# Decode stage of a hybrid decoder step: four row groups for the outer products, column groups for the k/q and attention products, and a fixed step for every piece

## The reference

```
# SSD, 16 heads of 64 rows x 128 columns, per sequence b
h   = h * exp(dt*A) + outer(dt*x, B)        # new state
y   = (C . h) + D*x
# gated DeltaNet (GDN), 8 heads of 128 x 128, per sequence b
S   = S * exp(g)
vn  = beta * (v - k . S)                    # k, q normalised
S   = S + outer(k, vn)
y   = q . S
# memory attention, 4 heads, 256 tokens, per sequence b
p   = softmax(q . K / sqrt(128));  y = p . V
```

## Time and profile before

| | |
|---|---|
| median of 3 runs | 1452.47 us (1449.58 to 1455.79) |
| profiled execution | 1452.82 us, of which the trace's span is 1450.9 us |
| PE matmul busy in the span | 1351.4 us (93%) |
| mean granted TensorE clock | 0.982 of full speed |
| decode stretch (from the end of the prompt's GDN work to the last projection matmul) | 887.9 to 1183.9 us: 296.0 us |

### The profile page before, as it was taken

How to read it: one execution, slowest core, us unless ns; L and a number is a source line. 1 busy time by engine, 2 the same in 40 slices (tenths; PEclk the granted TensorE clock), 3 DMA queues, 4 the chain that set the end, 5 groups by cost and what they waited for, 6 DMA issues and landing times.

```text
span 1450.9 us, 25445 instructions
## 1 busy us (share of the span) xinstructions
PE 1351.4 (93%) x10652; PEld 1292.0 (89%) x10652; DVE 738.1 (51%) x1040; ACT 558.5 (38%) x992; POOL 474.7 (33%) x424
## 2 busy tenths in 40 slices
PE   6999998899999999999999999899899979999993
PEld 6999998888898999989899899898896979999993
DVE  7754434555457474656547541568662154233224
ACT  6653333432354545454443543232112162233221
POOL 3030003333535253444435454785221041010003
PEclk9999999999999999999999999999999999999997
DMA  7324342112111121111111114245444414333322
GB/s 279 101 88 130 118 131 88 44 44 59 59 59 47 46 59 41 50 46 59 46 60 61 60 44 133 73 151 169 161 159 163 158 59 132 116 111 110 111 65 118
DMA packets 38819, 138.14 MB, mean 95 GB/s; under 512 B 4449, under 2 KB 5857, under 8 KB 38449
## 3 DMA queue, kind: packets, MB, share of 16 engines
q1 hardware_dynamic: 30384, 109.80, 24.1%
q10 hardware_dynamic: 8208, 26.22, 5.2%
q0 software_dynamic: 112, 0.50, 0.1%
HBM read 121.25 MB, written 15.24 MB: 94 GB/s over the span
## 4 chain that ended last, share of the span: by engine, by line
PE 69%; DVE 10%; issue 10%; POOL 5%; ACT 5%; DMA 1%; DVEq 0%; ACTq 0%; POOLq 0%; SPq 0%
PE ps L753 33%; PE ps L1056 15%; PE ps L645 13%; POOL w_lo L1946 3%; PE ps L701 2%; DVE conv_a L1628 2%; PE ps L705 2%; PE ps L1026 1%; ACT w_hi L1083 1%; PE ps L1009 1%; ACT L1083 1%; DVE h_lo L1503 1%; DVE fin L1934 1%; DVE d_v L1871 1%; DVE w_lo L1481 1%
## 5 line engine op out<-in xcount | busy, mean ns | idle before, releaser
L753 PE MATMUL ps<-h_hi,w_hi 128*128 128x260 f32 x1920 | 421.6, 301 | 26.8 <-DVE w_lo L1481 11.2
L753 PE MATMUL ps<-h_lo,w_hi 128*128 128x260 f32 x1920 | 390.0, 285 | 0.0
L753 PE MATMUL ps<-h_hi,w_lo 128*128 128x260 f32 x1920 | 389.8, 285 | 0.0
L1083 ACT ACTIVATE w_hi<-w_raw 128x512 fp32r<-128x512 f32 x352 | 213.2, 624 | 445.8 <-PE ps L753 254.2
L753 PEld LDWEIGHTS ps<-h_hi,w_hi 128*128 128x128 f32 x1920 | 301.2, 192 | 40.5 <-issue 32.1
L753 PEld LDWEIGHTS ps<-h_lo,w_hi 128*128 128x128 f32 x1920 | 300.1, 191 | 0.0
L753 PEld LDWEIGHTS ps<-h_hi,w_lo 128*128 128x128 f32 x1920 | 299.8, 191 | 0.0
L1946 POOL TENSOR_TENSOR w_lo<-w_raw,w_hi 128x512 fp32r<-128x512 f32 x152 | 206.9, 1365 | 270.7 <-ACT w_hi L1083 270.1
L1481 DVE TENSOR_TENSOR w_lo<-w_raw,w_hi 128x512 fp32r<-128x512 f32 x200 | 149.1, 767 | 234.3 <-ACT w_hi L1083 233.6
L1056 PE MATMUL ps<-y_hi,w_hi 128*128 128x260 f32 x640 | 129.0, 283 | 9.6 <-DVE y_lo L1918 5.6
L1056 PE MATMUL ps<-y_lo,w_hi 128*128 128x260 f32 x640 | 129.3, 283 | 0.0
(11 more groups left out here) (334 smaller groups left out, 1913.6 us busy)
## 6 DMA issues: line engine op xcount, KB each, us to landing
w_raw<-in_w_in SPq DMA_DIRECT2D x120, 512.0 KB, 3.6
w_raw<-in_w_out SPq DMA_DIRECT2D x40, 512.0 KB, 3.6
w_raw<-in_w_mem SPq DMA_DIRECT2D x16, 512.0 KB, 3.5
x_t<-in_x_t SPq DMA_DIRECT2D x8, 520.0 KB, 7.7
fin<-in_x_t SPq DMA_DIRECT2D x8, 520.0 KB, 4.5
out_y_t<-fin SPq DMA_DIRECT2D x8, 520.0 KB, 2.7
d_st<-in_st_ssd ACTq DMA_DIRECT2D x8, 512.0 KB, 4.5
out_s_ssd<-d_st ACTq DMA_DIRECT2D x8, 512.0 KB, 3.3
```

The source lines that it names most:

```text
L753: last = mm(out[:, hf, :], w[:, g % 2, P * (at_k % 8):P * (at_k % 8) + P], a[:, at_k, HALF * hf:HALF * hf + HALF], start=(at_k == 0 and j ...
L1083: return nc.scalar.activation(out, in_, func, **more)
```

## The change

The list `late` and its pauses are gone. Every decode piece gets a fixed step, counted from the start of tile 43 (`DEC_AT`), and the projection of tiles 19 to 58 is one run of items into which they are put. The last pieces stand at steps 201 to 218, in tiles 55 and 56; the eight SSD pieces follow each other every 7.5 steps from step 13 on, the four GDN pieces start at steps 82, 96, 113 and 127, the attention products at 140 to 168 and 183 to 201. Some loads are issued two steps behind the product that frees their buffer.

```diff
-POOL_TILES = (12, 50)
+POOL_TILES = (12, 46)
+DEC_AT = [(-40, "zero"), (-34, "bcols")] + [(9.8 + 0.2 * i, ("load", i)) for i in range(4)]
+DEC_AT += [(10, "consts"), (12, "bcast"), (13.2, "dtx"), (14.4, "rows"), (16, "gzero"), (17.4, ("cb", 0)), (34, "gcols"), (46.4, ("cb", 1)),
+           (60.2, "grows"), (62.6, "gss"), (63.4, "grk"), (65.2, "gcoef")]
+for _i in range(8):
+    DEC_AT += [(13 + 7.5 * _i, ("decay", _i)), (19.2 + 7.5 * _i, ("outer", _i)), (20.4 + 7.5 * _i, ("add", _i)), (22.2 + 7.5 * _i, ("ymul", _i)),
+               (23.6 + 7.5 * _i, ("store", _i)), (24.6 + 7.5 * _i, ("yred", _i)), (30.4 + 7.5 * _i, ("load", _i + 4))]
+for _t, _kq in enumerate((82, 96, 113, 127)):
+    DEC_AT += [(_kq, ("kq", _t)), (_kq + 2.2, ("vn", _t)), (_kq + 4.6, ("gouter", _t)), (_kq + 6.6, ("gadd", _t))]
...
+for _b, (_k, _v) in enumerate(zip((140, 142, 154, 156, 158, 160, 166, 168), (183, 184.2, 185.4, 186.6, 195, 197, 199, 201))):
+    DEC_AT += [(_k, ("attk", _b)), (_k + 2, ("load", 20 + _b)), (_v, ("attv", _b)), (_v + 2, ("load", 28 + _b))]
```

On PE, the rows dt*x, B, C, k and v are now turned by transposes into tiles whose rows lie in four groups of 32 partitions, with masks that make B and C block-diagonal for two sequences (`b_diag`, `c_diag`) and vn for four (`d_vbd`). An outer product is then four matmuls, each from one row group and into a PSUM bank of its own:

```diff
+                elif step == "outer":
...
+                    for j in range(4):
+                        last = one(side[j][:, 0:2 * P], dtx_rows[32 * j:32 * j + 2, i, :], b_diag[32 * j:32 * j + 2, i // 4, :, :].rearrange("p i n -> p (i n)"))
+                    last.then_inc(sem("d_outer"), 1)
...
+                    for i in range(4):
+                        for j in range(4):
+                            last = mm(side[0][32 * j:32 * j + 8, 0:P], kq_sel[:, t, j, i, :], d_st[:, (2 * t + i // 2) % 4, 4 * (i % 2) + j, :],
+                                      start=i == 0, stop=i == 3)
...
+                    for j in range(4):
+                        last = one(side[j], kq_rows[32 * j:32 * j + 4, t, :], d_vbd[32 * j:32 * j + 4, :, :].rearrange("p i v -> p (i v)"))
...
+                    for h in range(MEM_H):
+                        last = mm(side[0][32 * h:32 * h + DB, 0:MEM_T], q_sel[:, h, DB * b:DB * b + DB],
+                                  d_st[:, b % 4, 2 * h:2 * h + 2, :].rearrange("p m t -> p (m t)"), start=b == 0, stop=b == DB - 1)
...
+                    for m in range(2):
+                        for h in range(MEM_H):
+                            last = mm(side[3][32 * h:32 * h + DB, 0:P], p_sel[:, m, h, DB * b:DB * b + DB], d_st[:, b % 4, 4 * m + h, :],
+                                      start=(b == 0 and m == 0), stop=(b == DB - 1 and m == 1))
```

On POOL the outer product is gone; the decay stays, and seven memsets come in (two at step -40). On DVE the adds read the product from PSUM:

```diff
+                    V.tensor_tensor(st, st, ps[:, 4:8, 0:2 * P].rearrange("p j (i n) -> p j i n", i=2), ALU.add).then_inc(sem("d_new"), 1)
...
+                    V.tensor_tensor(by_group(d_tmp[:, :, :]), by_group(d_st[:, i % 4, :, :]), d_cb[:, :, :, :], ALU.mult).then_inc(sem("d_ymul"), 1)
```

More of the change, by code:

```diff
@@ L163, in spread, with spread_ssd @@
         upto = (i + 1) * len(side) // len(main)
-        out += [s for s in side[done:upto] if s != PAUSE]
+        out += side[done:upto]
         done = upto
     return out
-def paced(side):
-    out = []
+def spread_ssd(main, side):
+    padded = []
     for it in side:
-        step = f"{it[0]} {it[-1]}" if it[0] in ("ssd", "gdn", "att", "atty", "decgdn") else it[0]
-        out += [PAUSE] * PAUSES.get(step, 0) + [it]
-    return out
+        padded += [None] * (it in (("ssdend",),) or it[0] == "ssd" and it[2] == 1) + [it]
+    return [it for it in spread(main, padded) if it]
 def proj_items(first, last):
@@ L215, in timeline @@
     start = proj_items(a, b)
[L216 removed]
+    items += start[:FIRST] + spread_ssd(start[FIRST:], side)
     phases = {}
@@ L229, in timeline @@
     assert not phases
[L230 to L238, removed]
     items += spread(proj_items(NTILE - 1, NTILE), [("yhi", e) for e in range(ET - 4)])
     items += [("ylo", 0), ("ylo", 1), ("post", NTILE - 1, 0), ("post", NTILE - 1, 1), ("post", NTILE - 1, 2), ("ylo", 2), ("ylo", 3), ("out", 0, 0), ("post", NTILE - 1, 3),
-              ("out", 0, 1), ("post", NTILE - 1, 4), ("out", 0, 2), ("decgate", 2), ("ylo", 4), ("ylo", 5)]
+              ("out", 0, 1), ("post", NTILE - 1, 4), ("out", 0, 2), ("dec", "gate", 2), ("ylo", 4), ("ylo", 5)]
     items += spread([("out", 0, e) for e in (3, 4, 5)], [("yhi", e) for e in range(ET - 4, ET)])
@@ L444, in build @@
[L444 to L449, removed]
-    d_sv = r_side.place("d_sv", [P, 4])
-    d_n = r_side.place("d_n", [P, 2, ET, DB])
+    kq_cols = r_side.place("kq_cols", [P, 4, P])
+    d_vbd = at("d_vbd", [P, 4, P], F32, r_side.next - 4 * 4 * P)
+    kq_rows = r_side.place("kq_rows", [P, 4, P])
+    bv_rows = r_side.place("bv_rows", [P, 4, P])
@@ new lines, in build @@
+    d_diag = at("d_diag", [P, 320], F32, r_side.next)
+    d_sel = at("d_sel", [P, P], F32, r_side.next + 320 * 4)
+    d_tmp = r_side.place("d_tmp", [P, DB, P])
+    d_rq = r_side.place("d_rq", [P, GDN_H * DB])
+    d_dx = r_side.place("d_dx", [P, 8, DB])
+    d_sv = r_side.place("d_sv", [P, 4])
+    assert r_side.next <= r_side.start + (ET - 1) * NT * 4
+    r_b.reset()
+    s_cols = r_b.place("s_cols", [P, 12, P])
+    kq_sel = r_b.place("kq_sel", [P, 4, 4, 4, 8])
+    v_cols = at("v_cols", [P, 4, P], F32, conv_u_at)
@@ L503, in across, with groups, by_group, pairs_of @@
         return ap.unsqueeze(1).to_broadcast([ap.shape[0], m, ap.shape[1]])
+    def groups(t):
+        return t.rearrange("p (j r) -> p j r", r=32)
+    def by_group(ap):
+        return ap.rearrange("p (i j) n -> p j i n", j=4)
+    def pairs_of(ap):
+        return ap.rearrange("p h b -> p (h b)").rearrange("p (t i j) -> p t j i", t=4, j=4)
+    def cols_of(tile, first):
+        return tile.rearrange("p t (j r) -> p t j r", r=32)[:, :, :, first:first + 4]
     def chunk(c):
```

656 lines of the change are left out of this document (370 added, 286 removed).

## The result

The changed kernel takes 1387.97 us (median, 1386.41 to 1391.25), the kernel before 1452.09 in the same comparison: a ratio of 0.957 (95% interval 0.955 to 0.959). The forecast was 1421 with a range of 1395 to 1456, so the sign was right and the size was not: the change brings twice what was forecast, and more than the low end of the range.

What follows compares the result with a forecast made beforehand. PE was taken to set the pace, with 105.4 us of its 296.0 us decode stretch open to change; -18.9 + 3.4 - 9.3 - 5.0 - 2.0 = -31.8 took 1452.8 to 1421 us, range 1395 to 1456.

Steps and rivals of the forecast that it cites:

- decode products: Small decode matmuls on PE: partial overlap of row and column groups, 53.1 us in place of 72.0, -18.9.
- tile shapes: PE's changes of tile shape: 35 bursts of small tiles in place of 17, at 0.19 us each, +3.4.
- PE's waits: PE idle in the decode stretch: 20.3 us falls to 11 (range 4 to 20), -9.3.
- clock: TensorE clock in the decode stretch: fewer waits, fewer falls, half of the loss stays, -5.0 us.
- the end: Last tile: norm and gates move to tiles 55 and 56, off ACT while it rounds y, -2 us.
- the first term: Decode matmuls on PE: 46.1 us for six sums, between 23.2 (complete overlap) and 77.6 (none); -18.9 in all.
- The signs named for it: Chain pieces in the trace: `outer` at 1.15 right, 0.84 or 1.84 wrong; `attk` 1.15 against 0.46 or 1.84.
- The rival of complete overlap: Decode products on PE: groups overlap completely, 22.9 us less and 2 of waits back, 1400 us; chance 20%.
- the fourth term: TensorE clock: fewer waits bring fewer falls and half of the loss stays, -5.0 us (0 to -10).
- Groups that take turns: Decode products on PE: each group waits for the one before, +12.6, 1467 us; half of no overlap's 18%.
- no-change variant: Decode products on PE: no overlap, but waits fall as forecast, 1452.6 us; half of no overlap's 18%.
- Waits that move to DVE: SSD part: DVE takes POOL's place, splits come late, third and fourth terms (waits, clock) are lost, 1435 us; chance 17%.

Runs made afterwards that it cites:

- one group: Changed kernel with all four products of each set reading row group 0 or writing column group 0: 1450.18 us, ratio 0.999.
- by turns: Changed kernel with each outer product issued three times, group after group: 1392.37 us, ratio 0.959; for k/q products, the changed kernel's own order, 1387.97 us.
- in pairs: Changed kernel with k/q products issued two of one column group in a row, then the next group's, twice round: 1392.72 us in one execution.
- six in a row: Changed kernel with each outer product issued three times, six instructions for one row group before the next group's: 1410.72 us, ratio 0.972.
- the moved splits: Kernel before with GpSimd splitting low parts up to tile 46 instead of 50: 1456.95 us; changed kernel with the limit back at 50: 1389.14 us.
- A regular spread of the pieces: Changed kernel with decode pieces in the same order but at even distances from step 9.8 to 239.5: 1383.77 us, ratio 0.953.
- eight in a row: Changed kernel with k/q products issued eight instructions per column group and value products four, before the next group's: 1390.99 us, ratio 0.958.

## Why the prediction was wrong

Terms of the sum as the forecast had them, and as the two profiled executions show them:

| term | forecast (its bounds) | measured |
|---|---|---|
| decode products | -18.9 (-41.8 to +12.6) | 72.0 to 29.5: -42.5 |
| tile shapes | +3.4 | +2.4 |
| PE's waits | -9.3 (-16.3 to 0) | 20.3 to 3.5: -16.8 |
| clock | -5.0 (0 to -10) | 9.9 to 1.9: -8.0 |
| the end | -2 (0 to -4) | 0 |
| sum | -31.8 | -64.9 |

(29.5 is 23.5 for the six sums and about 6 for transposes and small products; the shapes are what is left, 231.1 - 190.6 - 29.5 - 3.5 - 1.9 = 5.6 in place of 3.2.)

**The step that failed** is the choice of a value between the bounds of the first term. The bounds were right at both ends: 77.6 without overlap (77.3 measured with one group) and 23.2 with complete overlap (23.5 measured), the lower one in part by luck. The ten bursts of `cb` and `outer` took 6.5 where it had 8.4, since it let the weight loads of the four groups follow each other, and in the trace they start within 0.02 us and last 0.18; the other bursts took 17.0 where it had 14.8, for the fixed part of each. I took 46.1, by the assumption that the second instruction of a product, which goes to the same group as the first, holds back the next group's. The signs named for it decide: `outer` 0.65, under even the 0.84 of the best case, and `attk` 0.55 against 0.46 and 1.15. The runs by turns, in pairs and in a row show what holds instead: an instruction for a busy group doesn't hold back what is behind it until four stand for the same group, one running and three waiting. With the order of the change (never more than two in a row) the limit never comes into play. So PE does not keep strictly to program order between groups, though the opening section says so of every engine: with six in a row the second group's first starts 0.54 us after the burst's start, the first group's fourth at 0.75.

The Trainium skill, TensorE: Matmul & The Clock Gate, Part 3 (Packing small matmuls), says that matmuls start and end strictly in program order. As a rule for when they start, the traces don't agree with it: eight instructions in two lengths and a fixed part leave no room for the third to wait behind the second. Its measured 3.07 for four row groups, with 512 columns, is near to what the runs gave: 1.92 / 0.65 = 2.95 for `outer`, with 256 columns, and 3.62 / 1.07 = 3.4 for `gouter`, with 512. Column groups gave 1.82 / 0.55 = 3.3 and 3.59 / 0.99 = 3.6.

**The rival of complete overlap** was the right mechanism, but at 1400 it was too slow by 12: 9.5 of that are waits (3.5 measured, where it kept the forecast's 11 and added 2 for DVE), 3 are the clock. DVE was hardly late: the add is 1.22, POOL or not, and the multiplication fell from 1.85 to 1.41, so seven and a half steps have some 5.9 us of DVE work where I had 6.4 (and 7.2 at worst), in PE's 6.3. The waits named one by one were over-counted: loads 3 and the vn chain 2 gave nothing, POOL's splits 0.3 for 2, DVE's splits 1.5 for 3 (and 1.0 for an add). That the waits go without the overlap too (0.15 us with one group) makes them a term of their own. Which part of the change takes them away is not separated: the moved splits and the steps set by hand are out, and the outer products that left POOL, `vn` in two operations and the new order of the pieces remain.

**The clock** was put down to waits alone in the fourth term. Its loss fell by 8.0 in place of 5.0, and the run with one group has next to no waits and loses 14 us to the clock. So falls stand behind a gap in PE's work and also, with no gap, behind bursts of products with two or four rows; shortening the bursts, which the first term counted only by its own length, kept the clock up as well. The kernel before has a fall of the second kind too: in the first window of the earlier trace rows PE is busy for all of its 29.9 us and the clock is 0.94. It falls behind the burst of 3.68 at 900.83, products with 8 rows (their row, then the window behind them):

```profile
L645 PE MATMUL ps<-ident_r,d_tmp 8*128 8x8 f32 x32 | 3.7, 252 | 0.0
```

```profile
905.00:910.00 5.00, 5.00 (x32) 5.00 (x31) 0.15 (x1) 0.41 (x1) 1.29 (x1) 0.66 0.34 105
```

Its other falls stand beside waits, and how its 9.9 divide was not tried.

**The end** gave nothing: the last roundings of y still come after the last projection, and the part behind the decode stretch is as long as before (267.2 us, and 267.0 before).

**The rivals that lost.** Groups that take turns: no, though its no-change variant, 1452.6, is what the kernel with one group gives (1450.18), so that part of the working stands: products up, waits down, nothing gained. Waits that move to DVE: 1.5 and 1.0 us in place of the 14.3 that this rival priced. The Trainium skill's rule on PSUM Bottleneck (TensorEngine Tiling (Array Packing)) is not seen in these traces: the add that reads PSUM kept to 1.20 to 1.22 us. What the rival said of DVE's splits is seen in the kernel before with the moved splits, where they came late and cost 6.7 us of waits.

**The range** ended at 1395, without the fast edge of the case of complete overlap, and that case itself kept the forecast's waits and clock, though products and clock go together here: shorter bursts leave fewer falls of the clock. Its low end should have been the sum of the best ends, 1452.8 - 41.8 + 3.4 - 16.3 - 10 - 4 = 1384.

## What to carry to other kernels

Small fp32 products between big ones are worth putting into four row or column groups: here 77 us of them became 24 (the products that they replaced were 72 with the small ones), issued by turns, so that no more than four instructions in a row go to one group. Where the bounds of an overlap are far apart, a value between them needs a row that shows it; without one, the forecast should be given as two cases, and effects that hang on the same cause (here the length of the bursts and the clock) should be summed within a case. A regular spread of the pieces did as well as steps set by hand.

## What the runs showed of the hardware that I had not expected

- Order within a burst: 32 instructions of 128 columns took 0.99 us by turns, 1.01 in pairs of products and 2.31 eight in a row; 24 of 256 columns took 1.51 by turns and 3.11 six in a row. In both runs in a row the next group starts when three instructions of the group before have yet to start, so a limit of four for each group, one running and three waiting. What makes this limit stays open.
- The clock without a gap in PE's work: behind most bursts of 3.1 to 3.7 us of products with two, four or eight rows, and behind three of ten of 1.92 us, it fell from 2.4 to 1.2 GHz for a few microseconds; behind bursts of 3.59 with 128 rows and 8 weight columns it stayed at 1.00. These bursts differ in more than their rows, and what about them decides was not separated.
- A DVE add of 1024 columns takes 1.22 us with one operand from PSUM, beside a busy POOL as well. With both in SBUF it takes 1.21 to 1.23 by itself and 2.20 to 2.91 beside POOL's splits and decays.
